# Splitting the value product of two attention branches into three reduced-precision products

## The chip, the cores and the metric

The kernel runs on one core of one Trainium2 chip. The metric is the device time of one execution in microseconds (us); the median of three runs is compared. Beside those runs one execution was taken by the hardware profiler; its times and its trace are what the rows further down show. The engines are named as the profile names them: PE (matrix products), PEld (its weight loads, which overlap PE), DVE, ACT and POOL (elementwise work), SP (issues transfers). POOL issues transfers too, on the software queue q0; SP's run on the hardware queue q1.

## The reference, cut to what matters

One inference step of a two-layer decoder for 512 prompt positions and 8 samples, all in float32. The first layer mixes by pooling, the second by three attention branches over one shared key/value. What the change touches is the attention of the prompt: in each of 16 heads and for the two long branches ("selected" and "window", 512 keys each), scores get a bias and a causal mask, a softmax, and the probabilities are multiplied with the values.

```python
s = jnp.einsum('bqgrd,bkgd->bgrqk', qg, kw).astype(jnp.float32) * SCALE + bias
p = jax.nn.softmax(jnp.where(vis, s, NEG_INF), axis=-1)
return jnp.einsum('bgrqk,bkgd->bqgrd', p.astype(vw.dtype), vw)
...
o = jnp.stack([o_cmp, o_slc, o_win], axis=2).reshape(B, T, N_BRANCH, N_HEADS, HEAD_DIM)
y = jnp.sum(gates[..., None] * o * jax.nn.silu(z), axis=2).reshape(B, T, D_ATT)
```

With 512 positions and eight blocks of 64 every block is selected, so both long branches are dense causal attention over 512 keys. The third branch ("compressed") has 31 keys.

## The kernel before

**Precision.** A float32 product on PE takes two recorded matmuls of two passes each. The large projections avoid it: each operand is split into a high part, rounded to the type fp32r, and the rest, the low part (also fp32r), and three one-pass products (high by high, low by high, high by low) are summed in PSUM. ACT writes the high part of a weight tile (`hi`, L938), DVE the low one (`lo`, L1274, raw minus high). The attention products are plain float32.

**A quad.** `quad` (L2027) is a quarter of one projection of 256 columns: 48 fp32r matmuls of 260 columns (L2023), in two halves of 24, `mm` 0 and 1. Between the halves it can run something else. `w_used` counts finished quads, and `hi` of the quad after next waits for it, because there are two weight buffers.

**The head loop.** Eight turns (`heads`), two heads each, 16 quads (slots s = 0 to 15) per turn, that is 128 quads; the first and, on ACT and DVE, the last turn are written out, the others are a loop. Beside the quads run six units u: u = 0, 1 are the compressed branch of the two heads, u = 2 to 5 the two long branches. For each unit, in the order of PE's program:
- `scores` (L2170) at the end of odd slot 3 + 2u: four float32 products of 512, 384, 256 and 128 columns, into the banks S[0], S[1], S[2] and the rest of S[1];
- DVE adds the bias and finds the maxima (`softmax`, L1637), ACT exponentiates (L1172), DVE forms the row factors, POOL multiplies the rows by them (L888);
- `turn` (L2187) between the halves of odd slot 5 + 2u: ten 128 x 128 transposes of the probabilities, into the same banks S;
- `turned`: ACT copies S[0] (512 columns) to the tile `probs_T` (L1185) while DVE copies S[1] (512) and S[2] (256) (L1663, L1664);
- `values` (L2201) after the quad of even slot 6 + 2u: for the key blocks j = 0 to 3, `v_group` block j by the transposed probabilities of the queries from 128 j on, so 512, 384, 256 and 128 columns, summed in the one bank O;
- DVE multiplies O with the gate `z_silu` (`values` on DVE, L1676, which raises `o_used`) and adds it to y (L1678). The next unit's `values` on PE waits for `o_used`.

The last unit is packed closer than the others: its `values(i, 5)` stands right behind slot 15, half a quad behind its `turn`. On DVE that slot holds `turned` of unit 5, then `values` of unit 4, then of unit 5. Behind it the next turn begins; POOL loads `v_group` and the bias for it (`head_loads`).

**After the heads** comes the sample stage. PE turns 16 sets of keys (`turn_set`, L2232), and DVE and ACT empty the banks (`rows_out`, L1704 and L1233). DVE's first `rows_out` stands behind a wait for two small transfers of POOL, `gates_sample` (L897) and `bias_sample` (L900). POOL issues them when the last quad is done. The compressed values of the samples, `vc_sample`, lie at the address `c_at`; they were loaded before the heads (L855, at the end of `gates_out`) and are first read by PE at L2281, in set 14. SP loads the sets through ten buffers.

## Time and profile before

| | us |
|---|---|
| median of three runs | 2509.56 |
| lowest and highest of them | 2508.77, 2512.83 |
| profiled execution, device time | 2503.51 |
| its span in the trace | 2501.5 |
| PE busy / weight loads busy | 2434.0 / 2269.8 |
| DVE / ACT / POOL busy | 900.9 / 737.4 / 371.1 |
| head loop, from the first quad to the last value product | 1242 to 2203.8 |
| sample stage, up to the last projection | 2203.8 to 2289.8 |

The span is what the trace covers; the device time has 2.0 us around it, and lies 6.05 us below the median of the other three runs. A busy time of an engine is a sum of recorded durations; matmuls overlap, so how long a piece of PE's work takes is read from starts, or from the chain of work that ended last, and not from the mean of one.

### The profile page before, as it was taken

The page shows a single profiled execution, that of the slowest core. Times are in us where ns is not written, and L with a number is a line of the kernel's source. Part 1 is how long each engine was busy: PE and PEld are TensorE (multiplying, and loading weights), DVE is VectorE, ACT ScalarE, POOL GpSimd, SP SyncE. Part 2 cuts the span into 40 slices and gives each one's busy share as a digit, 9 for nine tenths or more (in the row PEclk, how much of TensorE's full clock was granted, in tenths as well). Part 3 has the DMA queues.
Part 4 walks back from the last instruction along what each step waited for, and adds up shares of the span by engine and source line. Part 5 has one row for each costly group of instructions (what it writes and reads, how often), then busy time and mean ns, then how long its engine had stood idle before and what let it go on. Part 6 is the DMA issues. An engine that isn't in the chain of part 4 may idle for free.

```text
span 2501.5 us, 49140 instructions
## 1 busy us (share of the span) xinstructions
PE 2434.0 (97%) x20790; PEld 2269.8 (91%) x20790; DVE 900.9 (36%) x1664; ACT 737.4 (29%) x1222; POOL 371.1 (15%) x502
## 2 busy tenths in 40 slices
PE   6999999999999999999999999999999999998997
PEld 6888888888999999999999999999998989877997
DVE  1235111221163353333533333333333343444333
ACT  1125111111232231111533333343424333432222
POOL 2002000691000000010402111111111111123000
PEclk9999999999999999999999999999999999999999
DMA  9986787676553446663532222323232323388222
GB/s 328 341 293 192 247 268 228 197 228 218 186 176 114 135 152 210 195 194 111 160 90 80 77 86 77 86 68 89 73 85 68 94 68 94 109 329 301 86 91 88
DMA packets 322969, 394.67 MB, mean 158 GB/s; under 512 B 20919, under 2 KB 287415, under 8 KB 320755
## 3 DMA queue, kind: packets, MB, share of 16 engines
q1 hardware_dynamic: 307554, 328.72, 41.4%
q0 software_dynamic: 15216, 62.97, 7.5%
q8 instruction: 166, 2.72, 0.4%
q14 instruction: 33, 0.26, 0.0%
HBM read 371.01 MB, written 42.69 MB: 165 GB/s over the span
## 4 chain that ended last, share of the span: by engine, by line
PE 92%; DVE 2%; DMA 2%; ACT 1%; issue 1%; SPq 1%; ACTq 0%; POOL 0%; DVEq 0%
PE acc L2023 70%; PE work L1944 4%; PE out_acc L2201 3%; PE work L1884 2%; PE work L2170 2%; PE work L2187 1%; PE work L2232 1%; PE acc L1884 1%; PE work L1932 1%; PE out_acc L2198 1%; PE acc L2245 1%; DMA ada<-in_w_ada 1%; PE work L2164 1%; PE work L2109 1%; SPq L682 0%
## 5 line engine op out<-in xcount | busy, mean ns | idle before, releaser
L2023 PE MATMUL acc<-h_hi,w_hi 128*128 128x260 f32 x4896 | 1009.6, 287 | 10.4 <-issue 7.5
L2023 PE MATMUL acc<-h_hi,w_lo 128*128 128x260 f32 x4896 | 986.5, 283 | 0.0
L2023 PE MATMUL acc<-h_lo,w_hi 128*128 128x260 f32 x4896 | 984.8, 283 | 0.0
L2023 PEld LDWEIGHTS acc<-h_hi,w_hi 128*128 128x128 f32 x4896 | 753.6, 189 | 50.3 <-issue 47.7
L1274 DVE TENSOR_TENSOR w_lo<-raw,w_hi 128x1024 fp32r<-128x1024 f32 (+1 forms) x316 | 404.1, 1279 | 1020.6 <-ACT w_hi L938 1017.2
L2023 PEld LDWEIGHTS acc<-h_hi,w_lo 128*128 128x128 f32 x4896 | 755.1, 189 | 0.0
L2023 PEld LDWEIGHTS acc<-h_lo,w_hi 128*128 128x128 f32 x4896 | 754.2, 189 | 0.0
L938 ACT ACTIVATE w_hi<-raw 128x1024 fp32r<-128x1024 f32 (+1 forms) x316 | 332.7, 1053 | 1115.0 <-PE acc L2023 1106.1
L888 POOL TENSOR_TENSOR probs<-probs,row_stats 128x128 f32<-128x128 f32 (+3 forms) x128 | 110.2, 891 | 451.2 <-DVE row_stats L1651 451.2
L1944 PE MATMUL work<-rows_T_early,w_c_early 128*128 128x124 f32 x960 | 111.9, 275 | 0.7 <-ACT rows_T_early L982 0.7
L1944 PEld LDWEIGHTS work<-rows_T_early,w_c_early 128*128 128x128 f32 x960 | 109.5, 192 | 1.1 <-DVE rows_T_early L1349 1.1
L1172 ACT ACTIVATE probs<-probs,row_stats 128x128 f32<-128x128 f32 (+3 forms) x128 | 70.5, 552 | 70.0 <-DVE row_stats L1640 70.0
L1884 PE MATMUL work<-ada,c_cols 128*32 128x256 f32 x1024 | 69.8, 389 | 7.1 <-DMA ada<-in_w_ada 4.2
L2201 PE MATMUL out_acc<-probs_T,v_group 128*128 128x512 f32 (+3 forms) x256 | 76.0, 440 | 0.5
L2201 PEld LDWEIGHTS out_acc<-probs_T,v_group 128*128 128x128 f32 x256 | 46.1, 189 | 29.0 <-issue 18.0
L1663 DVE COPY probs_T<-work 128x512 f32<-128x512 f32 x32 | 22.1, 692 | 108.2 <-PE work L2187 108.2
L1208 ACT ACTIVATE z_silu<-acc 128x260 f32<-128x260 f32 x96 | 31.7, 381 | 80.4 <-PE acc L2023 80.4
L1637 DVE CUSTOM_DVE_ANT_0 probs<-work,bias_heads 128x128 f32<-128x128 f32 (+3 forms) x128 | 55.1, 487 | 0.0
L1932 PE MATMUL work<-consts,pages_early 128*128 128x128 f32 x256 | 36.9, 292 | 17.2 <-DMA pages_early<-in_cache_k_cmp 12.4
L1884 PEld LDWEIGHTS work<-ada,c_cols 128*32 128x32 f32 x1024 | 26.7, 109 | 28.1 <-DMA ada<-in_w_ada 6.2
L1932 PEld LDWEIGHTS work<-consts,pages_early 128*128 128x128 f32 x256 | 30.8, 150 | 22.6 <-issue 16.9
L823 POOL DMA_DIRECT2D out<-token_rows x25 | 15.3, 611 | 239.8 <-DVE token_rows L1576 239.8
(338 smaller groups left out, 1805.3 us busy)
## 6 DMA issues: line engine op xcount, KB each, us to landing
ada<-in_w_ada SPq DMA_DIRECT2D x192, 512.0 KB, 4.8
raw<-in_w_in_b SPq DMA_DIRECT2D x128, 512.0 KB, 3.9
raw<-in_w_in_a SPq DMA_DIRECT2D x64, 512.0 KB, 4.9
raw<-in_w_kv SPq DMA_DIRECT2D x48, 512.0 KB, 3.7
raw<-in_w_out_a SPq DMA_DIRECT2D x32, 512.0 KB, 3.8
raw<-in_w_out_b SPq DMA_DIRECT2D x32, 512.0 KB, 3.4
x_scr<-x POOLq DMA_DIRECT2D x2, 4160.0 KB, 12.9
pages_early<-in_cache_k_cmp SPq DMA_DIRECT2D x32, 256.0 KB, 4.3
```

Of the source, the lines that this page charges most:

```text
L888: last = nc.gpsimd.tensor_tensor(PR[:, at:at + w], PR[:, at:at + w], STAT[:, 8 + t:9 + t].broadcast_to([P, w]), ALU.mult)
L938: nc.scalar.activation(HI[j % 2][:, :, 0:n], RAW[j][:, :, 0:n], ACT.Copy).then_inc(hi_ready, 1)
L1172: last = nc.scalar.activation(PR[:, at:at + w], PR[:, at:at + w], ACT.Exp, bias=STAT[:, t:t + 1], accum_out=STAT[:, 4 + t:5 + t])
L1208: nc.scalar.activation(ZB[:, blk - 1, mm, half * HT:(half + 1) * HT], D[2 * mm + half][:, 0:HT], ACT.Silu)
L1274: V.tensor_tensor(LO[j % 2][:, :, 0:n], RAW[j][:, :, 0:n], HI[j % 2][:, :, 0:n].bitcast(F32), ALU.subtract).then_inc(lo_ready, 1)
L1637: last = V.tensor_tensor_reduce(PR[:, at:at + w], where[t], BH[:, hh, (3 - t) * P:512], 1.0, -3e38, ALU.add, ALU.max, STAT[:, t:t + 1])
L1884: last = mm_((D[2], D[3], S[2])[min(s, 2)][32 * g:32 * g + 32, 256 * half:256 * half + 256], CTF[:, k, :], ADA[b][:, g, :], start=(k == 0) ...
L1932: last = tr(S[g % 2][:, P * t:P * t + P], pg[:, t, P * g:P * g + P], ident)
L1944: last = mm_((S[2] if bank == 2 else D[3])[:, 0:NKV * NCMP], w1[kv][:, l, :], at, start=(l == 0), stop=(l == CL - 1))
L2023: last = mm_(out[half][0:n, 0:HT], part[slot][:, kk, cols_], src[:, k, half * HT:(half + 1) * HT], start=(first and part is HI and src is ...
L2170: last = mm_(where[t], qs(t), kt_[:, :, 0:P * (t + 1)].rearrange("p o t -> p (o t)"), start=True, stop=True)
L2201: last = mm_(O[:, P * j:512], VG[:, br - 1, j, :], PT[:, at:at + 512 - P * j], start=(j == 0), stop=(j == 3), skip_group_check=True)
```

## The change

In the two long branches (units 2 to 5) the key blocks 0, 1 and 2 are multiplied as split parts: high values by high probabilities, high values by low probabilities, low values by high probabilities, each fp32r. Block 3 (128 columns) stays one float32 product. Per unit PE has nine fp32r matmuls of 512, 384 and 256 columns and one float32 product, where it had four float32 products.

The parts are made as follows. The probabilities: ACT rounds all three banks (512, 384 and 256 columns) into `probs_T_hi`, DVE subtracts them from the banks into `probs_T_lo` (three instructions) and copies the last 128 columns into `probs_T_last`. PE's `scores` of the next unit now waits bank by bank for these subtractions. The values: once per turn, ACT rounds `v_group` blocks 0 to 2 of both branches (768 columns) at slot 2, DVE writes the low part in place at slot 3, and PE's `values` waits for it. The new tiles need room: `q_heads` moves down to `c_at`, where `vc_sample` was. So the load of `vc_sample` moves on POOL from before the heads to behind them, with a wait for the last value product.

```diff
+        PTH = place("probs_T_hi", [P, 1152], F32R)
+        PT3 = place("probs_T_last", [P, P])
+        PT = nc.alloc_sbuf_tensor_at("probs_T_blocks", [P, 512], F32, offset=cursor[0] - 1280 * 4)
...
-        cursor[0] = c_at + TS * P * 4
+        cursor[0] = c_at
         QS = place("q_heads", [P, 2, TP])
+        PTL = place("probs_T_lo", [P, 1152], F32R)
+        VGH = place("v_group_hi", [P, 2, NT - 1, P], F32R)
+        VGL = nc.alloc_sbuf_tensor_at("v_group_lo", [P, 2, NT, P], F32R, offset=x_at + 2 * 1280 * 4)
...
-                pool.dma_start(VCS[:, :, :], vcs_scr.rearrange("b p n -> p b n")).then_inc(s_cin[1], 16)
                 pool.wait_ge(s_gd, 16 * 12)
...
             nc.gpsimd.memset(PX[:, :], 0.0).then_inc(s_dm, 1)
+
+            pool.wait_ge(c_done, 48)
+            pool.dma_start(VCS[:, :, :], vcs_scr.rearrange("b p n -> p b n")).then_inc(s_cin[1], 16)
...
-                    nc.scalar.activation(PT[:, 0:512], S[0][:, :], ACT.Copy).then_inc(pt_ready, 1)
+                    for b, at, w in ((0, 0, 512), (1, 512, 384), (2, 896, 256)):
+                        last = nc.scalar.activation(PTH[:, at:at + w], S[b][:, 0:w], ACT.Copy)
+                        if b < 2:
+                            last.then_inc(pth, 1)
+                    last.then_inc(pt_ready, 1)
...
+                    if s == 2:
+                        act.wait_ge(hd_in, 64 * (i + 1))
+                        wait(act, c_done, 6 * i)
+                        nc.scalar.activation(VGH[:, :, :, :], VG[:, :, 0:NT - 1, :], ACT.Copy).then_inc(vg_hi, 1)
...
-                V.tensor_copy(PT[:, 512:1024], S[1][:, :])
-                V.tensor_copy(PT[:, 1024:1280], S[2][:, 0:256]).then_inc(pt2_ready, 1)
+                for b, at, w in ((0, 0, 512), (1, 512, 384), (2, 896, 256)):
+                    if b < 2:
+                        dve.wait_ge(pth, 2 * (4 * i + u - 2) + b + 1)
+                    else:
+                        dve.wait_ge(pt_ready, n + 1)
+                    last = V.tensor_tensor(PTL[:, at:at + w], S[b][:, 0:w], PTH[:, at:at + w].bitcast(F32), ALU.subtract)
+                    if b == 1:
+                        last = V.tensor_copy(PT3[:, :], S[1][:, 384:512])
+                    last.then_inc(pt2_ready if b == 2 else ptl, 1)
...
+                        if t:
+
+                            wait(pe, pt2_ready if t == 1 else ptl, 4 * i + u - 2 if t == 1 else 2 * (4 * i + u - 2) - (t == 3))
...
-                    for j, at in ((0, 0), (1, 512), (2, 1024), (3, 512 + 384)):
-                        last = mm_(O[:, P * j:512], VG[:, br - 1, j, :], PT[:, at:at + 512 - P * j], start=(j == 0), stop=(j == 3),
-                                   skip_group_check=True)
+                    pe.wait_ge(vg_lo, i + 1)
+                    for j, at in ((0, 0), (1, 512), (2, 896)):
+                        w = 512 - P * j
+                        for v, p in ((VGH, PTH), (VGH, PTL), (VGL, PTH)):
+                            mm_(O[:, P * j:512], v[:, br - 1, j, :], p[:, at:at + w], start=(j == 0 and v is VGH and p is PTH), stop=False, skip_group_check=True)
+                    last = mm_(O[:, P * 3:512], VG[:, br - 1, 3, :], PT3[:, :], start=False, stop=True, skip_group_check=True)
```

PE at the end of a turn of the head loop, the second half of slot 15 and the value product of unit 5, before:

```order
L2023 MATMUL acc<-h_lo,w_hi_54 128x260 x2
L2023 MATMUL acc<-h_hi,w_lo_56 128x260 x2
L2201 MATMUL out_acc<-probs_T,v_group 128x512
L2201 MATMUL out_acc<-probs_T,v_group 128x384
L2201 MATMUL out_acc<-probs_T,v_group 128x256
L2201 MATMUL out_acc<-probs_T,v_group 128x128
L129 UNCONDITIONAL_BRANCH
```

and in the changed kernel:

```order
L2053 MATMUL acc<-h_hi,w_lo_56 128x260 x2
L2238 MATMUL out_acc<-probs_T_hi,v_group_hi 128x512
L2238 MATMUL out_acc<-probs_T_lo,v_group_hi 128x512
L2238 MATMUL out_acc<-probs_T_hi,v_group_lo 128x512
L2238 MATMUL out_acc<-probs_T_hi,v_group_hi 128x384
L2238 MATMUL out_acc<-probs_T_lo,v_group_hi 128x384
L2238 MATMUL out_acc<-probs_T_hi,v_group_lo 128x384
L2238 MATMUL out_acc<-probs_T_hi,v_group_hi 128x256
L2238 MATMUL out_acc<-probs_T_lo,v_group_hi 128x256
L2238 MATMUL out_acc<-probs_T_hi,v_group_lo 128x256
L2239 MATMUL out_acc<-probs_T_last,v_group 128x128
L129 UNCONDITIONAL_BRANCH
```

The place is the same; three float32 products have become nine.

DVE at the same place, before: the copies of `turned`, then `values` of unit 4 (L1676, L1678) and of unit 5:

```order
L1274 TENSOR_TENSOR w_lo_55<-raw_49,w_hi_53 128x1024
L1663 COPY probs_T<-work 128x512
L1664 COPY probs_T<-work 128x256
L1676 TENSOR_TENSOR o_times_z<-out_acc,z_silu 128x512
L1678 TENSOR_TENSOR y<-y,o_times_z 128x512
```

and in the changed kernel:

```order
L1294 TENSOR_TENSOR w_lo_55<-raw_49,w_hi_53 128x1024
L1688 TENSOR_TENSOR probs_T_lo<-work,probs_T_hi 128x512
L1688 TENSOR_TENSOR probs_T_lo<-work,probs_T_hi 128x384
L1690 COPY probs_T_last<-work 128x128
L1688 TENSOR_TENSOR probs_T_lo<-work,probs_T_hi 128x256
L1703 TENSOR_TENSOR o_times_z<-out_acc,z_silu 128x512
L1705 TENSOR_TENSOR y<-y,o_times_z 128x512
```

Two instructions have become four in front of the product that raises `o_used` (L1676 before, L1703 now).

POOL behind the last turn of the heads, before:

```order
L129 COMPARE_AND_BRANCH
L896 MEMSET probs_cmp_spread 128x124
L897 DMA gates_sample<-gd_scr 128x3x1
L900 DMA bias_sample<-bd_scr 128x513
L906 TENSOR_TENSOR q_one_sample_164<-q_sample,consts 128x128
```

and in the changed kernel:

```order
L129 COMPARE_AND_BRANCH
L905 MEMSET probs_cmp_spread 128x124
L908 DMA vc_sample<-vcs_scr 124x8x128
L909 DMA gates_sample<-gd_scr 128x3x1
L912 DMA bias_sample<-bd_scr 128x513
L918 TENSOR_TENSOR q_one_sample_169<-q_sample,consts 128x128
```

The load of `vc_sample` now stands in front of the two small transfers, on the same queue, behind its wait.

## Rows read from the trace of the kernel before

**Rows 1.** The page, parts 1, 2 and 4: busy times, granted clock, chain.
```profile
PE 2434.0 (97%) x20790; PEld 2269.8 (91%) x20790; DVE 900.9 (36%) x1664; ACT 737.4 (29%) x1222; POOL 371.1 (15%) x502
...
PEclk9999999999999999999999999999999999999999
...
PE acc L2023 70%; PE work L1944 4%; PE out_acc L2201 3%; PE work L1884 2%; PE work L2170 2%; PE work L2187 1%; PE work L2232 1%; PE acc L1884 1%; PE work L1932 1%; PE out_acc L2198 1%; PE acc L2245 1%; DMA ada<-in_w_ada 1%; PE work L2164 1%; PE work L2109 1%; SPq L682 0%
```

**Rows 2.** Chain of work, 1400 to 1530 us: start, us, what, count.
```profile
1427.56 2.16 PE work L2170 x8
1429.72 5.75 PE acc L2023 x48
1435.47 0.06 issue
1435.52 2.40 PE out_acc L2201 x8
...
1476.14 2.85 PE acc L2023 x24
1479.00 2.16 PE out_acc L2201 x8
1481.15 0.61 issue
```

**Rows 3.** Chain of work, 1212 to 1227 us: float32 matmuls of 124 columns.
```profile
1212.50 7.14 PE work L1944 x64
```

**Rows 4.** Timeline, slots 14 and 15 of a turn: start, us, instruction [idle before].
```profile
1476.18 0.60 ACT L1185 ACTIVATE probs_T<-work 128x512 f32<-128x512 f32 x1 [0.36 <-PE work L2187]
1476.18 0.69 DVE L1663 COPY probs_T<-work 128x512 f32<-128x512 f32 x1 [3.83 <-PE work L2187]
...
1476.79 0.41 DVE L1664 COPY probs_T<-work 128x256 f32<-128x256 f32 x1
...
1477.12 0.68 DVE L1676 TENSOR_TENSOR o_times_z<-out_acc,z_silu 128x512 f32<-128x512 f32 x1
...
1478.84 2.32 PE L2201 MATMUL out_acc<-probs_T,v_group 128*128 128x512 f32 x8
```

**Rows 5.** Timeline, 1424 to 1448 us: DVE on PSUM by width, and `o_used`.
```profile
1427.60 1.06 ACT L938 ACTIVATE w_hi<-raw 128x1024 fp32r<-128x1024 f32 x1 [2.27 <-PE acc L2023]
1428.69 1.23 DVE L1274 TENSOR_TENSOR w_lo<-raw,w_hi 128x1024 fp32r<-128x1024 f32 x1 [2.94 <-ACT w_hi L938]
1429.84 0.28 DVE L1637 CUSTOM_DVE_ANT_0 probs<-work,bias_heads 128x128 f32<-128x128 f32 x1
...
1430.40 0.55 DVE L1637 CUSTOM_DVE_ANT_0 probs<-work,bias_heads 128x384 f32<-128x384 f32 x1
...
1434.69 0.69 DVE L1674 TENSOR_TENSOR y<-out_acc,z_silu 128x512 f32 x1
```

**Rows 6.** Groups on ACT, 1405 to 1512 us, shapes apart: busy, mean ns, idle before.
```profile
L1208 ACT ACTIVATE z_silu<-acc 128x260 f32<-128x260 f32 x12 | 4.0, 381 | 9.9 <-PE acc L2023 9.9
```

**Rows 7.** Chain of work, 2200 to 2345 us: into and out of the sample stage.
```profile
2202.56 4.82 DMA bias_sample<-bd_scr
...
2208.15 3.77 PE work L2232 x20
...
2275.89 7.83 DMA set_h<-in_cache_v_slc
```

**Rows 8.** Transfers by issue, whole span: count, KB each, us from issue to landing.
```profile
kc_sample_T<-kcs_scr POOLq DMA_DIRECT2D x1, 496.0 KB, 7.4
vc_sample<-vcs_scr POOLq DMA_DIRECT2D x1, 496.0 KB, 16.4
```

**Rows 9.** Timeline of POOL's issues, 1225 to 1270 us: the same two transfers.
```profile
1231.13 0.93 POOL L837 DMA_DIRECT2D kc_sample_T<-kcs_scr  x1 [0.60 <-issue]
...
1248.63 2.06 POOL L855 DMA_DIRECT2D vc_sample<-vcs_scr  x1
```

**Rows 10.** Transfer queues, 1258 to 1264 us: packets, MB, share of 16 engines.
```profile
q0 software_dynamic: 146, 0.37, 18.1%
```

**Rows 11.** Timeline, 2194 to 2240 us: POOL, DVE and PE behind the heads.
```profile
2201.76 0.80 POOL L897 DMA_DIRECT2D gates_sample<-gd_scr  x1
...
2203.80 0.69 DVE L1676 TENSOR_TENSOR o_times_z<-out_acc,z_silu 128x512 f32<-128x512 f32 x1 [2.66 <-PE out_acc L2201]
...
2208.15 3.77 PE L2232 MATMUL work<-consts,set_h 128*128 128x128 f32 x20 [3.13 <-DVE rows_T L1704]
```

**Rows 12.** Stretches: width, busy us of PE, PEld, DVE, ACT, POOL; PEclk; DMA share; GB/s.
```profile
2201.50:2210.00 8.50, 5.37 (x30) 4.34 (x29) 2.73 (x5) 3.42 (x7) 2.46 (x5) 0.86 0.84 275
2210.00:2220.00 10.00, 10.00 (x122) 7.15 (x121) 4.15 (x6) 3.58 (x6) 2.41 (x5) 0.95 1.05 402
```

**Rows 13.** Timeline, slot 2 of the next turn: where the split of the values goes.
```profile
1485.02 0.55 POOL L873 DMA_DIRECT2D vc_group<-vc_scr  x1
...
1493.59 1.06 ACT L938 ACTIVATE w_hi<-raw 128x1024 fp32r<-128x1024 f32 x1 [4.72 <-PE acc L2023]
...
1494.68 1.23 DVE L1274 TENSOR_TENSOR w_lo<-raw,w_hi 128x1024 fp32r<-128x1024 f32 x1 [4.56 <-ACT w_hi L938]
```

More of the change, by code:

```diff
@@ L323, in build @@
         PR = place("probs", [P, 1280])
-        PT = place("probs_T", [P, 1280])
+        PTH = place("probs_T_hi", [P, 1152], F32R)
+        PT3 = place("probs_T_last", [P, P])
+        PT = nc.alloc_sbuf_tensor_at("probs_T_blocks", [P, 512], F32, offset=cursor[0] - 1280 * 4)
         VG = place("v_group", [P, 2, NT, P])
@@ L502, in build @@
         b_done = sem("probs_turned")
+        pth = sem("probs_T_hi_parts")
+        ptl = sem("probs_T_lo_parts")
+        vg_hi = sem("v_group_hi_ready")
+        vg_lo = sem("v_group_lo_ready")
         pt_ready = sem("probs_T_ready")
@@ L1683, in heads @@
                         lo(Q_H + 4 * i + (s + 1) // 4, (s + 1) % 4)
+                    if s == 3:
+                        dve.wait_ge(vg_hi, i + 1)
+                        V.tensor_tensor(VGL[:, :, 0:NT - 1, :], VG[:, :, 0:NT - 1, :], VGH[:, :, :, :].bitcast(F32), ALU.subtract).then_inc(vg_lo, 1)
                     if s >= 4 and s % 2 == 0 and s < 16:
@@ L2156, in scores @@
                 wait(pe, pt_ready, n)
-                wait(pe, pt2_ready, 4 * i + max(0, u - 2))
+                if br == 0:
+                    wait(pe, pt2_ready, 4 * i)
                 qs = lambda t: QS[:, hh, P * t:P * t + P]
```

## The prediction, made before the changed kernel ran

> **What bounds the kernel now.** I read the page first, then the chain of work through two turns of the head loop and through the stage behind it, then the timelines at the places that the diff touches. The page says that PE is busy 97% of the span, at the full clock in every slice, and that the chain of work runs over PE nearly everywhere [rows 1]. So what PE saves is saved, unless something else then ends last. The chain inside a turn shows how full PE is: 48 matmuls of a quad in 5.75 us, a value product of 2.16 us, and hardly a gap [rows 2]. The 0.06 us in front of the value product at 1435.47 is one: there PE waits for DVE's product that raises `o_used` (DVE ends at 1434.69 + 0.69 = 1435.38, PE's first matmul starts at 1435.52), and the product then takes 2.40 instead of 2.16 [rows 2, 5]. So DVE is level with PE at some slots. Behind the heads PE really stands: the chain goes through POOL's load of `bias_sample` (4.82 us) and PE starts again at 2208.15 [rows 7].
>
> **Part 1: the value products.** A unit takes 2.16 us from start to start for 1280 columns in float32 [rows 2]; two records of two cycles per column are 2560 x 2 / 2.4 GHz = 2.13 us, so its eight records carry 3.4 ns each on top. Now 3 x (512 + 384 + 256) = 3456 columns pass once: 1.44 us at 2.4 GHz; and the last block keeps 128/1280 of 2.16, 0.216 us. What each fp32r matmul costs beyond its columns has no row at these widths. At 260 columns it is 5.75/48 = 119.8 ns against 108.3, so 11.5 ns [rows 2]. If that were proportional to the columns, the nine would take 3456 x 119.8/260 = 1.592 us; if fixed, 1.44 + 9 x 0.0115 = 1.544; at the 3.4 ns of the wide float32 records 1.471; with nothing at all 1.44. With the last block: 1.81, 1.76, 1.69, 1.66. Narrow float32 matmuls of 124 columns take 7.14/64 = 111.6 ns against 103.3, 8 ns more [rows 3], while wide ones pay 3.4, so it is not proportional; I take the fixed 11.5 ns of the nearest type. Gain 2.16 - 1.76 = 0.40 us in each of 8 x 4 = 32 units, **-12.8 us** (bounds -11.2 and -16.1). All of it is on PE, which sets the end.
>
> The Trainium skill (TensorE: Matmul & The Clock Gate, "Wait — 56ns, not 53.3ns?") puts warm matmuls at N / 2.4 GHz plus about 2.5 ns from start to start. By it a quad would take 48 x 110.8 ns = 5.32 us, which the row at 5.75 contradicts; its price here would be 1.44 + 0.02 + 0.22 = 1.68 us, a gain of 15.3 and a sum lower by 2.5 us.
>
> **Part 2: splitting the probabilities.** It starts when the turn is done. ACT: 601 ns for 512 columns, 381 for 260 [rows 4, 6], so some 490 and 380 ns for the new 384 and 256; about 1.4 us in all instead of 0.6. DVE needs ACT's first part: it begins 0.60 + 0.03 us later than now (0.03 as from L938's end to L1274 [rows 5]). On PSUM its widths 128, 256, 384 and 512 take 0.28, 0.41, 0.55 and 0.69 us, and successors start 0.08 us before the end [rows 4, 5]. Counted from ACT's start the three subtractions and the copy start at 0.63, 1.24, 1.71 and 1.91 and DVE is free for the next at 2.24; the copies were through at 1477.12 - 1476.18 = 0.94.
> - Slots 9, 11, 13: `scores` of the next unit follows 2.85 us behind the turn, and takes the banks in the order S[0], S[1], S[2]: S[0] is free at 1.32, S[1] and S[2] under 2.4, needed at 2.8, 3.7 and 4.3. Price nothing; the cover is half a quad. ACT and DVE are through before `hi` and `lo` of the slot's end come up.  The path DVE to `o_used` begins at `hi` behind the quad and is not lengthened, so the stalls at 1435.47 stay.
> - Slot 15: here it costs. DVE's order is `turned`, then the product that frees O (0.68 us), and `values(i, 5)` on PE waits for that. It will end at 1476.18 + 2.24 + 0.68 = 1479.10, PE starts 0.14 behind as at 1435.52, so 1479.24; PE was there at 1478.84 [rows 4]. A stall of 0.40 us in each of 8 turns, **+3.2 us**. Low bound 0.2 each (1.6), if the ends overlap more; high bound 0.8 (6.4), if DVE's instructions don't overlap across the new waits and each wait costs some 0.05.
>
> **Part 3: splitting the values.** Once per turn 768 columns on ACT, between 0.60 (512 wide) and 1.06 us (1024), and on DVE between 0.69 and 1.23. They stand behind `hi` and `lo` of slots 2 and 3, where both engines idle 4.72 and 4.56 us [rows 13]. The wait for the loads is covered too: POOL's last issue starts at 1485.02, ACT comes by at 1494.65 [rows 13]. Nothing, and nothing below nothing. What lies behind on ACT is `hi` of the next slot, which has those 4.7 us.
>
> **Part 4: the moved load.** Before the heads its removal frees a queue on which nobody waits: nothing. Behind them it stands in front of `bias_sample`. POOL now waits for the last value product, whose end DVE sees at 2203.80 [rows 11]; -0.40 and +0.40 of parts 1 and 2 leave it there. Then: issue of `vc_sample` 2.06 us (the similar `kc_sample_T` 0.93 [rows 9]), `gates_sample` 0.80 [rows 11], and `bias_sample` lands 4.82 us after its issue [rows 7]: 2203.80 + 2.06 + 0.80 + 4.82 = 2211.48 against 2202.56 + 4.82 = 2207.38. That is +4.1 us (+3.0 with the short issue). On top, `bias_sample` shares the software queue with 496 KB issued just before it. Alone such a load landed in 7.4 us once and in 16.4 once [rows 8]; in six microseconds of the latter the software queue moved 0.37 MB [rows 10], at which 508 KB take 8.2 us. If the data flow from about 2.6 us behind the issue, they end at 2214.6, and `bias_sample` right behind; that would be +8 instead of +4.1. If they use all 16 engines evenly as the 7.4 suggests, they are gone by 2211.2 and cost nothing more. I take 2.5 us between. PE's standstill also meets the clock: the granted clock was 0.86 and 0.95 in the stretches behind today's 3.13 us gap [rows 11, 12], and a longer gap adds some 0.4 us. **+7.0 us** (bounds +3.0 and +14). PE passes this on in full: it turns the sets at its own pace, and the stage ends 7.83 us of loads behind a buffer that PE frees [rows 7].
>
> The Trainium skill (DMA: Bandwidth & Descriptors, "Anatomy of one DMA — SWDGE (gpsimd) path") fits such a transfer as 2.0 us plus bytes / 436e3, which is 3.2 us here. Both rows are far above it. By it the queue would be clear before `bias_sample` comes, and part 4 would be 4.5 instead of 7.0.
>
> **Sum.** -12.8 + 3.2 + 7.0 = -2.6 us. On the profiled execution that is 2503.51 - 2.6 = 2500.9; on the median of the runs, which lies 6.05 us above it, **2507.0 us**.
>
> **Rivals.**
> 1. The queue does not hold `bias_sample` (part 4 is 4.1 + 0.4) and wide fp32r matmuls pay 3.4 ns, not 11.5 (gain 0.47 x 32 = 15.1): -15.1 + 3.2 + 4.5 = -7.4, so 2502.2. For it: the float32 rows, where wide ones pay less, and the 7.4 us. Against: the 260-wide row and the 16.4. Chance 0.24.
> 2. Slower: `bias_sample` waits until `vc_sample` has wholly landed. 16.4 us behind 2203.8 is 2220.2, and about 1 us more for its own data: +13.8, and the sum is -12.8 + 3.2 + 13.8 + 0.4 = +4.6, so 2514.2; here the other queue fills the DMA engines (share 1.05 [rows 12]), and with 20 us it is 2517.8. From a delay of 9.2 us on the change gains nothing. Against it: in the earlier place twelve small transfers stood before `vc_sample`. Chance 0.13.
> 3. The banks come free too late and `scores` waits 0.3 us in each of 24 slots, +7: 2514. It needs DVE 1.5 us later than I worked out at S[0]. Chance 0.03.
> 4. The fp32r matmuls of 256 to 512 columns run no faster than float32 ones: three products then cost three times one, tens of microseconds slower. The 260-wide rows speak against it. Chance 0.01.
>
> The forecast has 0.59.
>
> **How the numbers follow.** A measurement of this kernel can tell about 0.2%, 5 us, from no change. The forecast's own range, from the bounds of its parts taken together, is 2501 to 2513. Rival 1 reaches to about 2500, rival 2 begins at 2513. I give 2500.5 to 2514.0, leaving out the far ends of both. Faster by over 0.2% (under 2504.5): most of rival 1 and a little of the forecast, 0.27. Slower (over 2514.6): half of rival 2, rivals 3 and 4 and the forecast's edge, 0.13. Within: 0.60.
>
> **What would show it.** Step 1: the start-to-start time of a unit's ten value matmuls near 1.76 us (1.69 is rival 1). Step 2: a gap in front of `values(i, 5)` in every turn, released by DVE's product into `o_times_z`, and no wait of `scores` on DVE. Step 3: the idle time in front of `hi` at slots 2 to 4 shorter, and nobody waiting. Step 4: PE idle behind the heads about 10 us instead of 3.1, released through DVE by the landing of `bias_sample`; 7 would be rival 1, 17 rival 2. A quad that takes longer than 5.75 us, or a stall at slots 9 to 13, would make the prediction wrong in a way that it does not hold.

## The result, and the profile after

| | before | after |
|---|---|---|
| median of the runs (us) | 2509.73 | 2539.43 |
| lowest and highest | 2508.77, 2512.83 | 2535.18, 2543.93 |
| runs | 4 | 4 |
| span of the profiled execution | 2501.5 | 2533.2 |

The changed kernel is slower: 1.0119 of the time before, 95% interval 1.0106 to 1.0133. That is 29.7 us where the prediction had 2.6 us less, and it lies far outside the range that was given.

The difference of the spans, 31.7 us, divides by four points that both chains of work have:

| stretch | before | after | difference |
|---|---|---|---|
| up to the first quad of the heads | 1242.08 | 1244.21 | +2.1 |
| heads, first quad to the last quad's end | 959.5 | 969.9 | +10.4 |
| from there to PE's first turn of a sample set | 6.58 | 23.94 | +17.4 |
| all behind it | 293.35 | 295.2 | +1.85 |

So two places matter: the way out of the heads, and something inside them that more than ate the gain.

**The page of after**, parts 1, 2 and 4, answers [rows 1]. PE has 2 us more of busy time, but its share fell by a point; its last digits show a slice at 6 tenths, and the clock one at 8; `bias_sample` has entered the chain.

```profile
PE 2436.1 (96%) x20886; PEld 2290.5 (90%) x20886; DVE 930.6 (37%) x1736; ACT 764.2 (30%) x1294; POOL 371.7 (15%) x502
...
PE   7999999999999999999999999999999999968997
...
PEclk9999999999999999999999999999999999989999
...
PE 90%; DVE 3%; issue 2%; DMA 2%; ACT 2%; SPq 1%; POOL 0%; ACTq 0%; DVEq 0%; POOLq 0%
```

**The chain of work of after, one unit and the end of a turn** (start, us, what, count). It answers [rows 2].

```profile
1431.41 5.75 PE acc L2053 x48
1437.15 0.17 issue
1437.32 1.82 PE out_acc L2238 x9
1439.15 0.22 PE out_acc L2239 x2
1439.37 2.86 PE acc L2053 x24
...
1448.35 5.75 PE acc L2053 x48
...
1477.07 2.85 PE acc L2053 x24
1479.92 0.20 issue
1480.12 1.82 PE out_acc L2238 x9
1481.94 0.22 PE out_acc L2239 x2
1482.16 2.30 issue
1484.47 24.86 PE acc L2053 x192
```

Three things are to be read here.

- *The unit.* The value product takes 1.82 + 0.22 = 2.04 us, where it took 2.40 at this slot [rows 2]. These are the chain's pieces, which reach to the modelled end of a matmul; from the product's start to the next quad's start it is 1.80 us (1437.32 to 1439.12) where it was 2.15 (1435.52 to 1437.67). The gap ahead of it is 0.17 instead of 0.06. From quad to quad it is 1448.35 - 1431.41 = 16.94 us; before it was 17.19 (1429.72 to 1446.91). A unit gained 0.25 to 0.27 us, not 0.40.
- *The end of the turn.* PE stands 2.30 us between the last value product and the first quad of the next turn, where it stood 0.61 [rows 2]. The six ends of a turn inside the loop show 2.30, 2.21, 2.10, 2.10, 1.73 and 2.27; before they showed 0.61, 0.60, 0.52, 0.56, 0.55 and 0.52. Together 12.7 against 3.4 us.
- *The quads behind it.* 192 matmuls take 24.86 us; before, the same 192 took 23.32 (chain, 1481.76). The table of stretches (width, busy us of PE, PEld, DVE, ACT, POOL; granted clock; DMA share; GB/s) shows why: the granted clock went down to the lower level, half, for a part of them.

```profile
1484.00:1488.00 4.00, 3.53 (x18) 3.54 (x19) 1.23 (x1) 0.00 (x0) 1.67 (x3) 0.63 0.88 265
```

This happened at four of the six ends of a turn, with about 1.5 us of delay each time. In the kernel before it happened at none. The length of the gap alone does not decide it: the clock fell behind the gap of 2.10 us and not behind that of 2.27.

The sum of the heads closes: 24 units at -0.27 are -6.5; the eight last units +0.6 (a chain of 0.20 + 2.04 where 2.16 stood); the gaps +9.3; the clock +6.1. That is +9.5 against the measured +10.4.

**What PE does in the 2.30 us.** The records of PE's sequencer for the loop's branch (count, then least, median and greatest duration in ns, and the start in us), first of after, then of before:

```profile
L129 PEldq COMPARE_BRANCH  x1: 3899/3899/3899, 1480.3 to 1480.3; - x1
```

```profile
L129 PEldq COMPARE_BRANCH  x1: 3408/3408/3408, 1478.1 to 1478.1; - x1
```

The sequencer is the part of PE that hands instructions on to the array. The rows are read so: the branch begins when the sequencer has handed on the last instruction of the turn, and PE works off meanwhile what was handed on. Before, 1478.1 + 3.41 = 1481.5 and PE restarts at 1481.76; the queued work lasted until 1481.15, so 3 us of the branch were hidden. After, 1480.3 + 3.90 = 1484.2, restart 1484.47, and the queued work ended at 1482.16: 1.9 us hidden. The branch can't begin before the waits of `values(i, 5)` have passed. In after the last of them comes late, as the timeline of DVE shows:

```profile
1477.74 1.16 DVE L1688 TENSOR_TENSOR probs_T_lo<-work,probs_T_hi 128x512 fp32r<-128x512 f32 x2 [4.22 <-ACT probs_T_hi L1198]
...
1479.01 0.42 DVE L1688 TENSOR_TENSOR probs_T_lo<-work,probs_T_hi 128x256 fp32r<-128x256 f32 x1
1479.34 0.68 DVE L1703 TENSOR_TENSOR o_times_z<-out_acc,z_silu 128x512 f32<-128x512 f32 x1
```

`o_used` rises at 1480.02. Before it rose at 1477.80 [rows 4], a whole microsecond ahead of the product, and the branch began 0.3 us later. This lateness of 2.2 us is what I had priced at 0.40.

Of the 9.3 us of longer gaps, 2.0 are longer branch records (22.2 us in all six, 20.2 before). The other 7.4 are cover that is gone: 1.86 us at this end instead of 3.05.

The Trainium skill (Runtime: NRT & Kernel Launch, "Instruction fetch mechanics") says: "A taken branch whose target isn't in the current 2-page window forces a DMA fetch of the target page before execution can continue". The branch records of 3.3 to 3.9 us agree with that, and the trace shows a transfer in each. Here are the queues from 1480.3 to 1484.2, the branch above (packets, MB, share of 16 engines); nothing else moved:

```profile
q8 instruction: 1, 0.02, 1.5%
```

In all 66 ends of a turn, six in each of eleven kernels (before, after and the nine below), PE restarts 0.23 to 0.39 us behind the branch's end, and a packet of this queue begins 0.85 to 1.6 us behind the branch's start. In the 60 branches under 4 us the end comes 2.3 to 3.0 us behind that packet's start. In the six of 4.6 to 5.3 us (e1, e2 and e6 below) two such packets begin 0.3 to 0.5 us apart. A branch that is not taken, the last of the loop, took 0.08 us. So a branch's length goes with its instruction transfers; the rows don't say for which engine a packet is, and no run changed that.

**Behind the heads**, the chain of after, to be held against [rows 7]:

```profile
2216.43 1.16 issue
2217.59 2.09 POOL vc_sample L908
2219.68 0.75 POOL gates_sample L909
2220.43 16.81 DMA bias_sample<-bd_scr
...
2238.01 4.53 PE work L2269 x20
```

The transfers by issue there (size, us from issue to landing), and the stretch with PE standing; the clock was at its lower level from about 2222.3 to 2242.8 us:

```profile
vc_sample<-vcs_scr POOLq DMA_DIRECT2D x1, 496.0 KB, 18.4
bias_sample<-bd_scr POOLq DMA_DIRECT2D x1, 256.5 KB, 16.8
```

```profile
2222.00:2242.00 20.00, 3.99 (x19) 3.99 (x20) 2.26 (x4) 1.19 (x2) 0.00 (x0) 0.51 1.07 277
```

The two issues cost what was worked out (2.09 + 0.75 for 2.06 + 0.80). POOL begins them 1.16 us behind the last value product, which the sum did not have. And `bias_sample`, 256 KB, took 16.8 us instead of 4.82, and lands 1.3 us behind `vc_sample`. Of the 17.4 us, 12.0 are this landing and 5.4 the wait and the issues ahead of it.

### The profile page after: what moved, and what is told of

Read it like the earlier page. It is cut to its first block, busy times and chain, and to the rows that moved or that the text cites. A ratio compares the mean times of both kernels' runs of the same rounds, so it can differ in the third digit from the quotient of the medians.

```text
span 2533.2 us, 49569 instructions
## 1 busy us (share of the span) xinstructions
PE 2436.1 (96%) x20886; PEld 2290.5 (90%) x20886; DVE 930.6 (37%) x1736; ACT 764.2 (30%) x1294; POOL 371.7 (15%) x502
## 4 chain that ended last, share of the span: by engine, by line
PE 90%; DVE 3%; issue 2%; DMA 2%; ACT 2%; SPq 1%; POOL 0%; ACTq 0%; DVEq 0%; POOLq 0%
PE acc L2053 69%; PE work L1974 4%; PE work L1914 2%; PE out_acc L2238 2%; PE work L2204 2%; PE work L2221 1%; PE work L2269 1%; PE acc L1914 1%; PE work L1962 1%; PE out_acc L2232 1%; DMA bias_sample<-bd_scr 1%; PE acc L2282 1%; DMA ada<-in_w_ada 1%; PE work L2195 1%; PE work L2139 1%
## 5 line engine op out<-in xcount | busy, mean ns | idle before, releaser
L1688 DVE TENSOR_TENSOR probs_T_lo<-work,probs_T_hi 128x512 fp32r<-128x512 f32 (+2 forms) x96 | 50.3, 552 | 123.2 <-ACT probs_T_hi L1198 123.2
L1198 ACT ACTIVATE probs_T_hi<-work 128x512 fp32r<-128x512 f32 (+2 forms) x96 | 40.2, 493 | 80.2 <-PE work L2221 80.2
L890 POOL TENSOR_TENSOR probs<-probs,row_stats 128x124 f32<-128x124 f32 x16 | 6.2, 390 | 313.5 <-DVE row_stats L1675 313.5
L994 ACT ACTIVATE rows_T_early<-work 128x512 f32<-128x512 f32 x32 | 19.1, 596 | 105.7 <-PE work L1962 105.7
```

Of the source, the lines that this page charges most:

```text
L1688: last = V.tensor_tensor(PTL[:, at:at + w], S[b][:, 0:w], PTH[:, at:at + w].bitcast(F32), ALU.subtract)
```

## The experiments

Two theories were to be tested. **Theory L**: at the end of a turn PE's branch takes 3.3 us and more, and the value product covers it only from the moment its last wait passes; whoever makes that wait late lays the branch open, and the low clock can follow the gap. **Theory Q**: the load of 124 partitions in front of `bias_sample` holds it up. Rivals are that fp32r products or the longer program cost the time, and that `bias_sample` is slow for another reason.

### e1: the load behind bias_sample

```diff
-            pool.wait_ge(c_done, 48)
-            pool.dma_start(VCS[:, :, :], ...)
             pool.dma_start(GD[:, :], ...)
             pool.dma_start(BD[:, :], bd_scr).then_inc(s_bd, 16)
+            pool.wait_ge(c_done, 48)
+            pool.dma_start(VCS[:, :, :], ...)
```

> The changed kernel with one edit: on POOL the wait for the last value product and the load of vc_sample stand behind the issue of bias_sample instead of in front of it. Theory Q (bias_sample was held in the software queue behind the data of vc_sample): bias_sample lands about 5 us after its issue instead of 16.8, PE restarts about 6.6 us after the last quad instead of 23.9, and the time falls by 17 us to about 2522. Rival theory I (what delays it is POOL's own wait and its issue time of 2.1 us, and the crowded DMA engines do the rest): only the 4 us of wait and issue come back, bias_sample still takes over 12 us to land, about 2535.

Measured: 2530.23 us (2522.18 to 2531.26), ratio to before 1.0082 (1.0065 to 1.0098), span 2520.2. The chain:

```profile
2214.45 5.95 DMA bias_sample<-bd_scr
...
2221.17 4.53 PE work L2269 x20
```

The load still lands in 19.6 us, and nobody waits for it. PE restarts 7.7 us behind the last quad instead of 23.9. The order of two issues was worth 16 us of the standstill. The span shows 13.0 of them, since in this execution two branches took 4.8 and 5.1 us and PE stood 3.4 and 3.7 us behind the product, where it had stood 1.7 and 2.3. The medians differ by 9 and miss the expected 2522 by 8 us; what the other three executions lost is in no trace.

### e5: the load alone, on the kernel before

```diff
-                pool.dma_start(VCS[:, :, :], ...)
...
             nc.gpsimd.memset(PX[:, :], 0.0).then_inc(s_dm, 1)
+            pool.wait_ge(c_done, 48)
+            pool.dma_start(VCS[:, :, :], ...)
             pool.dma_start(GD[:, :], ...)
```

> The kernel before with one part of the change alone: the load of vc_sample moved from before the heads to behind them, in front of gates_sample and bias_sample, with its wait. Theory Q: the whole cost of this part appears alone, PE restarts 23 to 24 us after the last quad instead of 6.6, +17 us, about 2527. Rival: the load is late in the changed kernel only because something else there also slowed; then this run is within 5 us of before plus 4, about 2514. The gap at the end of a turn of the head loop stays at 0.6 us.

Measured: 2526.85 us (2523.13 to 2528.44), ratio 1.0064 (1.0047 to 1.0081), span 2525.0.

```profile
2212.87 16.40 DMA bias_sample<-bd_scr
```

With float32 products everywhere and PE's heads as before, the same load costs the same: 16.4 us for `bias_sample`, a restart 23.3 us behind the last quad. So this part of the loss, +17 us, is the moved load and nothing else. (The gaps at the turn ends were 0.86 to 0.95 with branches of 3.68 to 3.78 us: the branch varies by some tenths between kernels with the same waits.)

### e2: the same place, two pieces

```diff
-            pool.dma_start(VCS[:, :, :], ...)
+            pool.dma_start(VCS[0:112, :, :], ...)
+            pool.dma_start(VCS[112:124, :, :], ...)
```

> The changed kernel with the load of vc_sample (124 partitions) issued as two, of 112 and 12 partitions, at the same place. If the 18.4 us of that load come from its being spread over few DMA engines (124 partitions do not divide by 16), the piece of 112 is spread over 16, both land in under 12 us, bias_sample behind them in under 9 instead of 16.8, and the time falls by 6 to 9 us, about 2531. If the load is evenly spread already and only the crowd of the other queue slows it, nothing changes beyond 1 us more of issue time, about 2540.

Measured in one run: 2525.03 us, span 2522.9, which is 10.3 us under the span of after.

```profile
vc_sample<-vcs_scr POOLq DMA_DIRECT2D x1, 448.0 KB, 4.7
...
bias_sample<-bd_scr POOLq DMA_DIRECT2D x1, 256.5 KB, 6.8
```

Nine tenths of the bytes land in 4.7 us once they are 112 partitions instead of 124 (4.7 and 6.3 us in e10 and e9), and `bias_sample` behind them takes 6.8 instead of 16.8. So it is neither the bytes nor the queue's order that costs 10 us, but how 124 partitions are carried. The Trainium skill (DMA: Bandwidth & Descriptors, "Why a DMA increments its semaphore by 16 and not by 1") takes for a transfer the largest number of engines up to 16 that divides the outer size of both its sides: 16 for 112 partitions, 4 for 124. The two durations agree with that; the same passage names an exception on trn2 with all 16 for some direct copies, which they speak against.

The queue rows support it without counting engines. First 2222 to 2234 us of e1, where the load of 124 partitions had the software queue to itself, then 2207 to 2212 us of e10, the two pieces with part of `bias_sample`:

```profile
q0 software_dynamic: 506, 0.50, 20.1%
```

```profile
q0 software_dynamic: 251, 0.73, 45.5%
```

Four engines of 16 can show 25% at most. The first share stays under it, the second does not. But the packets differ too, 1.0 KB each against 2.9, and no run tells the number of engines from the size of the packets.

### e3b: float32 products, DVE late in slot 15

The copy of S[1] in slot 15 is done three times more on the kernel before, each waited for. Nothing of the result changes.

```diff
                 dve.wait_ge(c_done, n)
+                if u == 5:
+                    for _ in range(3):
+                        o(V.tensor_copy(PT[:, 512:1024], S[1][:, :]))
                 V.tensor_copy(PT[:, 512:1024], S[1][:, :])
```

> The kernel before with three idle repeats of DVE's 512-wide copy in slot 15 (unit 5), each waited for, some 2.2 to 2.4 us more on DVE in front of the product that raises o_used; PE's program is untouched. Theory L (the branch at the end of PE's loop starts only when the wait of values(i,5) on o_used has passed, and takes 3.3 to 3.9 us, so it is no longer hidden behind the matmuls): PE's branch record starts about 2.3 us later behind the turn than in the kernel before, the gap at the loop's end grows from 0.6 to 1.5 us or more beside a stall of 1.3 in front of the value product; about 2.3 us in each of 6 turns and 1.3 in two, +16 us, and up to 1.7 us more in each turn in which the clock drops: 2526 to 2534. Rival theory C (the gap of 2.2 us in the changed kernel comes from the longer code of its loop body): the gap stays under 1.0 and only the stall of 1.3 appears eight times, about 2520.

Measured: 2520.79 us (2518.55 to 2523.09), ratio 1.0053 (1.0036 to 1.0070).

```profile
1482.82 2.39 PE out_acc L2204 x8
1485.21 1.70 issue
```

```profile
L129 PEldq COMPARE_BRANCH  x1: 3688/3688/3688, 1482.9 to 1482.9; - x1
```

This is the test of Theory L without any fp32r product. The branch begins right at PE's last wait (1482.9), the product hides 2.3 us of it, and the gap is 1.70 (the six: 1.70, 1.33, 1.63, 1.39, 1.64, 1.33) against 0.52 to 0.61. It is the gap that decides between the theories, and the mechanism is shown. The time does not decide: 2520.8 is what the rival gave, and 5 us under the range of Theory L (in the spans the run is 15.0 us above before, in the medians 12.6). The clock did not fall at any turn end here, so the gaps of 1.3 to 1.7 us did not bring it; in after it fell at four of the six.

### e6: after, with the load behind and `o_used` raised first

DVE's product of unit 4 in slot 15 goes ahead of the subtractions of unit 5 (its sum into y stays behind them).

```diff
+                    if s == 15:
+                        values(i, 4, 0)
                     if s >= 9 and s % 2 == 1:
...
-                        values(i, (s - 8) // 2)
+                        values(i, (s - 8) // 2, 1 if s == 16 else 2)
```

> The changed kernel with vc_sample behind bias_sample (as e1_vc_behind) and one edit on DVE: in slot 15 the product of unit 4 that raises o_used stands in front of the subtractions of unit 5 (its addition to y stays behind them). Theory L: PE's branch in that slot now waits for the last subtraction only, some 0.6 us earlier; the stall of 0.2 us in front of values(i,5) goes and the gap of 2.2 shrinks to 1.7 to 1.9, 3 to 5 us less than e1_vc_behind, about 2526. Theory C: the gap stays 2.2 and only the stall goes, 1.5 us less, about 2528.

Measured: 2517.75 us (2511.71 to 2520.03), ratio 1.0034 (1.0025 to 1.0044). 12.5 us under e1, where 3 to 5 were expected, but still slower than before. The two spans differ by 3.5 us; the rest lies in executions without a trace.

```profile
1480.86 1.58 PE out_acc L2247 x9
1482.44 0.22 PE out_acc L2248 x2
1482.66 3.00 issue
```

```profile
L129 PEldq COMPARE_BRANCH  x1: 4674/4674/4674, 1480.7 to 1480.7; - x1
```

The stall ahead of the product is gone; the gap behind it is not (3.00, 3.26, 1.58, 3.00, 1.56, 2.00). PE's last wait is now for the last subtraction, which ends at 1480.34, so the branch starts at 1480.7, 0.16 us ahead of the product's piece in the chain; and it took 4.7 us here. Raising `o_used` early was the wrong cure: the split itself ends too late for a unit that closes the turn. The branch's own duration (3.4 to 4.9 us within this one kernel) is a second matter; it goes with the packets of the instruction queue, as shown above. The clock fell behind the gaps of 3.00 and 3.26 at the first two ends and not behind the other 3.00.

### e7 and e8: the last value product behind the next turn's first quad

In e7 (after, with the load behind) and e8 (the kernel before) `values(i, 5)` moves behind quad 0 of the next turn, so that a quad whose data are long there stands last before the branch.

```diff
+                    if s == 0 and not (isinstance(i, int) and i == 0):
+                        values(i - 1, 5)
...
-                values(i, 5)
             looped(pe, o, 8, heads)
+            values(7, 5)
```

> The changed kernel with vc_sample behind bias_sample, and values(i,5) on PE and DVE moved behind the first quad of the next turn, so that no wait on DVE stands between the last quad and the branch. Theory L: the branch starts while half a quad is still queued and the gap falls to under 1 us, the clock stays at full, and the stall is gone; against e1_vc_behind 6 x 2 us of gaps, 8 x 0.2 of stalls and 5 or more us of clock come back, 18 us, about 2512. Theory C: the gap stays near 2 us, about 2528.

> The kernel before with the same move of values(i,5) behind the first quad of the next turn. Under both theories the gap of 0.55 us can fall by at most itself, 6 times: 0 to -3 us, 2507 to 2510. It tells how much of e7_pipe comes from the move and how much from the split value products, which should be 8 us (32 units of 0.26).

Measured: e7 2511.69 us (2507.64 to 2515.71), ratio 1.0013 (1.0004 to 1.0023); e8 2516.28 us (2513.41 to 2518.79), ratio 1.0031 (1.0019 to 1.0042).

The time of e7 is the expected 2512, but neither gap is small. The chain books the first 0.76 us of each gap on ACT's `z_silu`, here at the first end of e8:

```profile
1483.44 0.19 ACT z_silu_sample L1210
1483.63 1.16 issue
```

```profile
L129 PEldq COMPARE_BRANCH  x1: 3836/3836/3836, 1480.7 to 1480.7; - x1
```

PE's last quad ends at 1482.86 and PE restarts at 1484.79, 1.93 us later. `z_silu` is through at 1483.63, so it does not hold PE; the branch ends at 1484.54. The whole gaps are 1.93, 1.55, 1.62, 1.50, 1.43 and 1.46 us in e8, and 2.01, 1.38, 1.44, 1.48, 1.64 and 1.61 in e7. That is 6.1 us more than in the kernel before, most of the 8 us by which e8 is slower, where 0 to 3 us less were expected. For e7 it is shorter than in after (2.30 to 1.73), and the clock fell at one end only, behind 2.01 us. No wait on DVE stands between the quad and the branch now, yet the branch begins only 2.2 us ahead of the quad's end at every end of both kernels, where 3.05 to 3.1 were covered before. Why it does not begin sooner was not tested.

On equal footing (e7 against e8) the split is worth 4.6 us, even with the load of `vc_sample` at its late place.

### e9: three units split, the one that ends a turn not

Unit 5 stays one float32 product, as in the kernel before; units 2 to 4 are split. The load goes behind `bias_sample`, in two pieces.

```diff
+                elif u == 5:
+                    for j, at in ((0, 0), (1, 512), (2, 1024), (3, 512 + 384)):
+                        last = mm_(O[:, P * j:512], VG[:, br - 1, j, :], PT5[:, at:at + 512 - P * j], ...)
```

> The changed kernel with the split only for units 2 to 4 (24 of 32 units). Unit 5, whose value product is the last work of a turn on PE, stays one float32 product of 2.16 us. The load of vc_sample goes behind that of bias_sample, as two loads of 112 and 12 partitions. Theory (the float32 value product is what covers PE's jump back at the end of a turn: 2.8 us from the jump's start to the product's end; and the three products save only 0.27 us of chain per unit): the gap at the loop's end goes back to 0.55 to 0.95 us, no low clock behind it, 24 units at -0.27 us give -6.5 us, and the start of the compressed queries is within 1 us of the kernel before: about 2503 us, 0.3% under the kernel before. Rival (the jump itself takes longer in a longer loop body, whatever covers it): the jump's record is over 3.7 us in most turns, the gap stays over 1.3 us, and the time is 2508 us or more.

Measured: 2506.99 us (2504.20 to 2507.88, 11 runs), before 2508.89 (21 runs), ratio 0.9993 (0.9984 to 1.0002), span 2503.0. That is 32 us under the changed kernel, the best of all kernels tried, and not told apart from the kernel before.

```profile
1479.32 2.15 PE out_acc L2245 x8
1481.47 0.62 issue
1482.10 23.34 PE acc L2063 x192
```

The gap is back at 0.62 (the six: 0.62, 0.94, 1.08, 1.07, 0.77, 0.47, behind branches of 3.3 to 3.9 us), the clock stays up, and 192 matmuls take 23.34 again. From the first quad to the last of the heads it is 955.2 us against 959.5: -4.3. The 24 split units give -6.5 of it, and the gaps take back 1.6; 0.6 is left over. The rival is half right: with the cover restored, the branch was still 0.2 to 0.55 us longer than before at four of the six ends. Behind the heads PE restarts after 7.69 us instead of 6.58 (`bias_sample` 5.93). The forecast of 2503 was 4 us too low: it counted nothing for these two, and nothing for the 1.8 us later start of the heads and the 2.9 us more behind the restart, which the trace shows and I can't explain (the profiled execution of before lies 6 us under the median of its runs, so differences of this size between two traces carry little).

### e10: e7 with the load in two pieces

```diff
-            pool.dma_start(VCS[:, :, :], ...)
+            pool.dma_start(VCS[0:112, :, :], ...)
+            pool.dma_start(VCS[112:124, :, :], ...)
```

> The kernel of e7_pipe (values(i,5) multiplied behind the first quad of the next turn, the load of vc_sample behind that of bias_sample), with vc_sample loaded as two pieces, of 112 and of 12 partitions. Theory (the load of 124 partitions runs on few engines and holds the queue and the engines it shares with bias_sample): the wait for bias_sample is 4.8 to 5.2 us instead of 6.1, vc_sample lands within 8 us of its issue instead of 18 to 19, and the time is 1 to 4 us under e7_pipe, 2508 to 2511 us. Rival (behind bias_sample the load disturbs nobody): bias_sample at 6.1 us as in e7_pipe and the same time within 1 us.

Measured: 2510.99 us (2508.22 to 2514.15), ratio 1.0012 (1.0003 to 1.0021), 0.7 us from e7.

```profile
2205.12 7.26 DMA bias_sample<-bd_scr
```

The load landed in 4.7 and 6.3 us, as expected, but `bias_sample` in 7.26 instead of the hoped 4.8 to 5.2. The rival's time holds, within 1 us of e7, though it too expected a shorter landing (6.1): once the load is behind `bias_sample`, its shape hurts nobody. Why `bias_sample` takes 5.1 to 7.3 us in these kernels and 4.82 in the one before is open.

## Why the prediction was wrong, point by point

**The step that failed is part 2 at slot 15.** It priced DVE's later end as a stall of 0.40 us and nothing else, +3.2 us; it cost 18.2, since the same wait also holds back the loop's branch. Part 4 was too small (+17.4 for +7.0) and part 1 too large (-8.6 for -12.8). The three make +27.0 of the 31.7 us between the spans; 0.8 in the heads and the 3.95 before and behind the two stretches are not explained. In the order of the steps:

*What bounds the kernel.* Right as far as it went: PE was the bound in a turn. It overlooked one row that it had itself: 0.61 us of "issue" at 1481.15 [rows 2], the only idle time in the row that nothing explained. A number without a releaser on the engine that sets the end is a question: what is hidden there, and how much of it? The sequencer's records held the answer, 3.4 us of branch at every turn's end, of which 3.05 us were covered (1478.1 to 1481.15).

*Part 1, the value products.* The mechanism was right; the term was mis-sized, -8.6 (32 units at -0.27) instead of -12.8. The starts of the nine fp32r matmuls show the price per matmul nearly as worked out. The timeline of PE in slot 15:

```profile
1480.12 0.47 PE L2238 MATMUL out_acc<-probs_T_hi,v_group_hi 128*128 128x512 f32 x1 [0.20 <-issue]
1480.43 0.39 PE L2238 MATMUL out_acc<-probs_T_lo,v_group_hi 128*128 128x512 f32 x1
...
1480.88 0.34 PE L2238 MATMUL out_acc<-probs_T_hi,v_group_hi 128*128 128x384 f32 x1
...
1481.78 0.38 PE L2239 MATMUL out_acc<-probs_T_last,v_group 128*128 128x128 f32 x2
```

From start to start a 512-column matmul takes 0.22 to 0.23 us, one of 384 columns 0.18, one of 256 columns 0.12; with 11.5 ns over the columns they would be 0.225, 0.172 and 0.118. Only the first takes more, 0.31 (+0.08). The whole product is read at slot 10, to the start of the next quad, of after and then of before:

```profile
1439.12 0.49 PE L2053 MATMUL acc<-h_hi,w_hi 128*128 128x260 f32 x2
```

```profile
1437.67 0.48 PE L2023 MATMUL acc<-h_hi,w_hi 128*128 128x260 f32 x2
```

That is 1.80 us where 1.76 was worked out, against 2.15: 0.35 of the 0.40 are there. What was missing is the entry. From the start of the last pair of the quad to the product's start it is 0.56, 0.54 and 0.46 us in the three slots, where it was 0.45, 0.43 and 0.35: 0.11 more each time. DVE isn't its cause at slot 10: its product into y ends at 1437.07, ahead of the quad's end at 1437.15. I did not find what is. So a unit gained 0.25 to 0.27.

*Part 2, splitting the probabilities.* Its working held to a hundredth: from ACT's start (1477.11) to DVE's product (1479.34) it is 2.23 us, worked out 2.24. `scores` never waited for a bank, so rival 3 fell. The stall in the terms of the sum, from the half quad's start to the product's start, was 0.35 for 0.40 (1477.07 to 1480.12, before 1476.14 to 1478.84); the chain shows 0.20 of it as idle. What failed is that I took DVE's path to `o_used` as a matter of PE's next instruction alone. I asked who waits for DVE, and not what is queued behind the waiting instruction on PE's sequencer: the branch. This step was priced at +3.2 and cost 2.8 of stalls + 9.3 of gaps + 6.1 of clock, 18.2 us; 2.0 of the gaps are longer branches, for which no run shows that the late wait is the cause. e3b shows the later wait alone, without the low clock, and e9 shows it undone.

*Part 3, splitting the values.* Right: ACT's part takes 0.83 us at slot 2, and nobody waited.

*Part 4, the moved load.* The term was +7.0 and measured +17.4. I named the right mechanism as rival 2 ("waits until `vc_sample` has wholly landed", chance 0.13) and chose the middle between 7.4 and 16.4 us of landing. Neither of the two rows was "alone": the other queue had a share of 41.5% beside the 7.4 us (1232 to 1238.5 us of before) and of 41.7% beside the 16.4 (1250 to 1266). What differs is the shape, which the list of POOL's order and the kernel show: `kc_sample_T` goes to 128 partitions, `vc_sample` to 124. In the eleven kernels the first landed in 7.2 to 8.0 us, the second, where it was one load, in 16.4 to 19.6. So the row with the same tile was the nearer one; it came out at 18.4. e5 shows the term alone and e2 that the shape of the load is its cause. Even rival 2's time, 2514 to 2518, did not reach the result, because it had the heads at -9.6 us and they came out at +10.4.

*The range* was built from bounds of the terms that I had, and not from all of them: added up they give -11.5 to +9.2 us, 2498 to 2519, wider than the 2501 to 2513 that I called their sum. 2539 lies outside both. No bound covered a wait that the sum did not know of.

## What to carry to other kernels

In this kernel the work before a loop's branch covered the branch only from the moment that its own last wait had passed. Whoever makes that wait later pays at every turn, and no busy time shows it: read the idle time behind the last instruction of a turn and the sequencer's branch records before any change there. Early data for the last work is not enough by itself: with a quad of short matmuls there (e7, e8) only 2.2 us were covered, with the float32 product (before, e9) 3.05 and more. A load that is moved in front of another on the same queue should be judged by the landing times of loads of the same shape, partitions included, and put behind whatever is awaited. And a product that is cheaper by columns still pays at its entry: 0.11 us ahead of it and 0.08 in its first matmul here.

## What the runs showed of the hardware

- A loop's branch on PE took 3.3 to 3.9 us in 60 turns and 4.6 to 5.3 in six, in kernels whose bodies differ by a few instructions; not taken, it took 0.08. In each of the 66 a packet of the instruction queue begins 0.85 to 1.6 us behind the branch's start, in the six long ones two of them. PE restarts 0.23 to 0.39 us behind the branch's end at all 66.
- The lower clock, half, followed the gap on PE at four of six turn ends in after (gaps of 1.7 to 2.3 us), with about 1.5 us lost each time; in e3b (1.3 to 1.7) at none. Over all kernels it followed 16 of 24 gaps of 1.8 to 3.9 us and none of the shorter ones.
- A 496 KB load of 124 partitions landed in 16.4 to 19.6 us, one of 128 partitions and the same size in 7.2 to 8.0, 448 KB of 112 partitions in 4.7 to 6.3; what stood behind the first on the queue took 16.4 and 16.8 us instead of 4.8.
- fp32r matmuls with 128 rows and 512, 384 or 256 columns start 0.23, 0.18 and 0.12 us apart; the first of a group takes 0.08 more.
